# Where the batches of the second expert table, the norms and the routing pieces stand in a two-block transformer kernel on one core

## The reference, cut to what matters

```
qp = h @ w_pq;  sc = qp . sub_keys                 # 8 heads, 2 x 128 keys
s1, i1 = top_k(sc[0], 16);  s2, i2 = top_k(sc[1], 16)
top_s, top_c = top_k(s1[:, None] + s2[None, :], 16)
expert = e1 * 128 + e2                             # 8 x 16 rows of 16384, for each token
gate = softmax(top_s)
u = peer_u[expert];  w = gate * gelu(h . u)        # first table
y = sum(w * peer_v[expert])                        # second table
```

## Time and profile before

| | us |
|---|---|
| median of 3 runs | 2858.24 |
| lowest, highest | 2852.95, 2862.33 |
| the profiled execution | 2858.05 |
| its span, first to last instruction | 2856.2 |
| end of half 1's dense work on TensorE (last `key_scores`), in the trace | 2021.9 |
| windows of the last three rows of Rows 2 | `pq` of half 0, `pq` of half 1, `band` of half 0 |

### The profile page before, as it was taken

How to read it: one execution, slowest core, us unless ns; L and a number is a source line. 1 busy time by engine, 2 the same in 40 slices (tenths; PEclk the granted TensorE clock), 3 DMA queues, 4 the chain that set the end, 5 groups by cost and what they waited for, 6 DMA issues and landing times.

```text
span 2856.2 us, 26891 instructions
## 1 busy us (share of the span) xinstructions
PE 2056.2 (72%) x9570; PEld 1438.5 (50%) x9570; DVE 1378.4 (48%) x3142; ACT 417.0 (15%) x1058; POOL 1103.9 (39%) x1089
## 2 busy tenths in 40 slices
PE   8899899999889859786989999888520013323555
PEld 6788688876558648664767754446300000000111
DVE  3210256013327998966664345114479977564100
ACT  2311221012422122112000113311100000000000
POOL 1000011000003445545554543432565557777665
PEclk9899989989779969988999989989755556555677
DMA  6254359434227969988999987876787789999998
GB/s 232 74 155 141 103 208 347 152 96 133 71 89 290 348 229 342 348 318 323 362 406 349 384 310 288 292 279 225 285 327 281 289 303 363 363 364 370 384 361 329
DMA packets 214727, 779.13 MB, mean 273 GB/s; under 512 B 23892, under 2 KB 26516, under 8 KB 213572
## 3 DMA queue, kind: packets, MB, share of 16 engines
q0 software_dynamic: 155136, 564.97, 52.6%
q1 hardware_dynamic: 57272, 207.44, 20.6%
q10 hardware_dynamic: 2187, 5.01, 0.5%
HBM read 770.75 MB, written 6.58 MB: 272 GB/s over the span
## 4 chain that ended last, share of the span: by engine, by line
PE 52%; issue 15%; POOL 15%; DVE 11%; DMA 4%; ACT 2%; another core or an unknown queue 1%; ACTq 0%; DVEq 0%; POOLq 0%; SPq 0%
PE bank L546 39%; POOL main L489 15%; PE bank L710 4%; PE bank L649 2%; PE bank L665 2%; DMA main<-in_peer_v,idxT 2%; PE bank L614 2%; DMA main<-in_peer_u,idx 1%; DVE main L1405 1%; PE bank L656 1%; DVE small L1362 1%; PE bank L622 1%; DVE dots L1405 1%; DVE small L1359 1%
## 5 line engine op out<-in xcount | busy, mean ns | idle before, releaser
L546 PE MATMUL bank<-main,ring 128*128 128x256 f32 x4864 | 1085.3, 385 | 40.3 <-DVE main L1558 16.4
L546 PEld LDWEIGHTS bank<-main,ring 128*128 128x128 f32 x4864 | 932.6, 193 | 199.8 <-issue 45.1
L489 POOL DMA_INDIRECT main<-in_peer_v,idxT x512 | 527.6, 1031 | 499.0 <-PE bank L710 312.2
L489 POOL DMA_INDIRECT main<-in_peer_u,idx x512 | 539.8, 1054 | 465.3 <-DVE dots L1405 192.7
L710 PE MATMUL bank<-main,score_a 128*32 128x512 f32 x2048 | 358.8, 816 | 407.6 <-DMA main<-in_peer_v,idxT 377.0
L710 PEld LDWEIGHTS bank<-main,score_a 128*32 128x32 f32 x2048 | 73.7, 133 | 655.5 <-issue 654.3
L1405 DVE CUSTOM_DVE_ANT_0 main<-main 128x1024 f32<-128x1024 f32 x256 | 313.7, 1225 | 186.1 <-DMA main<-in_peer_u,idx 171.7
L1405 DVE CUSTOM_DVE_ANT_0 main<-main,h_a 128x1024 f32<-128x1024 f32 x256 | 313.6, 1225 | 97.2 <-DMA main<-in_peer_u,idx 69.3
L969 ACT ACTIVATE main<-bank 128x256 f32<-128x256 f32 (+4 forms) x346 | 146.6, 439 | 870.6 <-PE bank L546 708.1
L546 PE MATMUL bank<-ring,main 128*128 128x512 f32 (+3 forms) x624 | 239.4, 543 | 1.8 <-DMA ring<-in_w_stream 1.1
L482 POOL DMA_DIRECT2D main<-in_w_ada x48 | 25.5, 536 | 447.2 <-DVE main L1578 447.2
(11 more groups left out here) (221 smaller groups left out, 1363.5 us busy)
## 6 DMA issues: line engine op xcount, KB each, us to landing
ring<-in_w_stream SPq DMA_DIRECT2D x370, 512.0 KB
main<-in_w_ada POOLq DMA_DIRECT2D x48, 512.0 KB, 7.4
main<-in_peer_u,idx POOLq DMA_INDIRECT x512
main<-in_peer_v,idxT POOLq DMA_INDIRECT x512
main<-in_sub_keys SPq DMA_DIRECT2D x2, 1024.0 KB, 9.3
main<-rows_d SPq DMA_DIRECT2D x1, 1536.0 KB
main<-in_xT ACTq DMA_DIRECT2D x1, 1024.0 KB, 5.0
main<-in_memT POOLq DMA_DIRECT2D x1, 1024.0 KB, 8.8
```

Of the source, the lines that this page charges most:

```text
L489: gp.indirect_dma_start(rows_buf[:, slot, :], None, table, bass.IndirectOffsetOnAxis(ap=where, axis=0)).then_inc(landed[slot], 16)
L546: ins = pe.matmul(o, lhsT, rhs, **kw)
```

## The change

- `HEAD, PAIR, TAIL` go from 2.3, 3.4, 1.9 to 2.6, 3.8, 2.2: dots and batches are planned farther apart.
- On TensorE a tick now looks `LATE` = 8 us behind the clock, and a new `fill()` looks `EARLY` = 14 us ahead of it. `fill()` stands in `spread` before the wait for `diag_ready`, in each attention behind the second score product, and in front of the wait for `h2_ready`. The first batch of each tile comes `FIRST` = 24 us later.
- On VectorE and ScalarE no expert work is put in inside a norm (`spread`, `norm_std`).
- `route(n)` becomes a generator of six pieces. A routing that stood whole behind dot 8 of sixteen now has a piece behind each of dots 6 to 11, each due 1.3 us after its dot.

```diff
-    HEAD, PAIR, TAIL = 2.3, 3.4, 1.9
+    HEAD, PAIR, TAIL = 2.6, 3.8, 2.2
...
+            LATE, EARLY = 8.0, 14.0
+
             def tick(us):
                 clock[0] += us
                 if experts_now[0] is not None:
-                    experts_now[0].until(clock[0])
+                    experts_now[0].until(clock[0] - LATE)
+
+            def fill():
+
+                if experts_now[0] is not None:
+                    experts_now[0].until(clock[0] + EARLY)
...
                 norms[0] += 1
+                fill()
                 pe.wait_ge(S["diag_ready"], norms[0])
...
                 sums(KB)
                 spread()
-                tick(8.0)
+                fill()
+                clock[0] += 8.0
...
+                        if i == 1:
+                            fill()
...
-                        yield pace.batch(CG * t + q)
+                        yield pace.batch(CG * t + q) + (0.0 if q else FIRST)
...
                 mark("h2")
-                tick(6.0)
+                clock[0] += 6.0
+                fill()
...
                 norms[0] += 1
-                evacuated(sums_out + 1)
+                ve.wait_ge(S["lin_evacuated"], sums_out + 1)
...
-                    route(r0)
-                    yield pace.dot(n0)
-                    route(r0 + 1)
+                    for r in (r0, r0 + 1):
+                        for _ in route(r):
+                            yield pace.dot(n0)
+                    routing = None
...
-                        if j % TOPK == 8 and n // TOPK + 2 < r0 + TH * HEADS:
-                            route(n // TOPK + 2)
+                        if j % TOPK == 6 and n // TOPK + 2 < r0 + TH * HEADS:
+                            routing = route(n // TOPK + 2)
+                        if j % TOPK >= 6 and routing is not None:
+                            yield pace.dot(n) + 1.3
+                            next(routing, None)
```

More of the change, by code:

```diff
@@ L713, in combine @@
                 last.then_inc(S["v_used"], 1)
+            FIRST = 24.0
             def experts():
@@ L958, in _, with ready @@
             lin = [0]
-            def ready(n=1):
+            def ready(n=1, between=True):
                 lin[0] += n
-                experts_now.until(pace.lin[lin[0] - 1])
+                if between:
+                    experts_now.until(pace.lin[lin[0] - 1])
                 ac.wait_ge(S["lin_ready"], lin[0])
@@ L980, in norm_std @@
                 norms[0] += 1
-                b = ready()
+                b = ready(between=False)
                 if norms[0] > 1:
```

12 lines of the change are left out of this document (11 added, 1 removed).

## The result

| | before | changed |
|---|---|---|
| median, us | 2860.28 (4 runs) | 2916.22 (4 runs) |
| lowest, highest | 2852.95, 2865.84 | 2905.73, 2922.46 |
| ratio | | 1.0192, 95% interval 1.0169 to 1.0214 |
| the profiled execution, its span | 2858.05, 2856.2 | 2922.46, 2920.4 |
| end of half 1's last key scores | 2022.0 | 2033.2 |

The change costs 1.9%. Forecast were 2876 us: slower, as it came out, but the time lies 40 us above it and 14 above the range. In the profiled executions dense work ends 11.2 us later and the part behind it is 52.9 us longer.

A forecast was written before the change was run, and what follows sets the result against it. VectorE was taken to set the pace up to `out`, gathers and routings the end. Dense work ending 35 us earlier and 53 us more gathering gave 2858.05 - 35 + 53 = 2876 us, range 2843 to 2902.

The forecast's parts named there:

- Term 1: Half 1 up to `out`: fewer dots and one routing fewer due on VectorE shorten TensorE's waits, -30 us.
- the 92%: VectorE's busy share up to `out`, taken as too saturated for splitting the routing to gain anything there.
- Term 2: Later routings and bursts: shorter wait at `down` (-6), `mem` net -1; -7 us in all.
- Term 3: Batches' own TensorE time: six batches leave dense work (-11.5), one is covered in a norm (-2); -13 us.
- Term 4: TensorE waits for second-table rows in `norm2`, `cq`, `h2` and `o2`; +20 us, bounds +8 to +30.
- Term 5: `pq`: 18 half 1 gathers no longer run beside its weight stream; -5 us.
- Term 6: Behind dense work: 37 more gathers are left to do; +53 us, bounds 46 to 60.
- Sum 15 + 4 + 6 + 12 - 16.6: New row waits in `norm2`, `cq`, `h2`, `o2`, less the old row waits that go: +20 us.
- the term's own rule: New waits come wherever three or four batches stand in a row, since only two batches' rows are held.
- A: Rival, faster: VectorE stops being late up to `out`, waits in `mem`, `cq` and `o2` go; 2845 us, chance 0.20.
- B: Rival, no change: half the 37 gathers is hidden or dense work ends 50 us earlier; about 2858, chance 0.20.
- C: Rival, clearly slower: gathers take longer where weights stream; 2898 us, chance 0.12.

The follow-up runs named there:

- e3: Kernel before with only the routing split into six pieces; 2833.21 us, ratio 0.9912.
- e1: Kernel before with only the slower pace (HEAD, PAIR, TAIL 2.6, 3.8, 2.2); 2860.45 us, ratio 1.0005.
- e14: Changed kernel without its TensorE placement (LATE and FIRST 0, fills empty); pace, norms and pieces kept; 2866.08 us, ratio 0.9979 to the kernel before.
- e4: Kernel before with only expert work kept out of norms on VectorE and ScalarE; 2859.86 us, ratio 0.9991.
- e15: Changed kernel with old PAIR and TAIL, LATE and FIRST 0, fills kept; 2837.69 us, ratio 0.9882 to the kernel before.
- e13: The changed kernel itself, measured again in a later sitting; 2916.99 us, ratio 1.0168 to the kernel before.
- e12: Changed kernel with FIRST = 0 alone, LATE and fills kept; ratio 1.0053 to the kernel before.
- e10: Changed kernel with LATE and FIRST 0, fills kept; ratio 1.0006 to the kernel before.
- e17: Changed kernel without the fill behind the attentions' second score product, other fills kept; 2898.41 us, ratio 1.0115 to the kernel before.
- e18: Changed kernel with fills only in the attentions, none in norms or at h2; 2911.97 us, ratio 1.0177 to the kernel before.
- e2: Changed kernel with the old pace (HEAD, PAIR, TAIL 2.3, 3.4, 1.9); 2909.93 us, ratio 1.0185 to the kernel before.
- e11: The same kernel as e14, run in a sitting with faster gathers; 2809.06 us, ratio 1.0042 to the kernel before.

## Why the prediction was right or wrong

**Term 1, up to `out`: right in size, in part by luck.** `out` ends 33.3 us earlier (1247.8 to 1214.5), a batch (1.9) of it moved on: 31.4 for 30.4. The wait in `norm0`, which I said would nearly stay, went from 10.9 to 6.9. VectorE does 103 dots up to there for the 119 of the earlier trace rows. But the sentence "The six pieces alone bring nothing here" was wrong. The stretch takes 327.3 us before, 321.3 with the pieces alone (e3), 299.5 with the pace alone (e1) and 293.3 with both and the norms (e14), and the norms alone change nothing (e4, 327.4). So the pace is worth 27.8 us, 25.9 without the batch, and the pieces the other 6, against the 92%. Here the sentence of the Trainium skill that I set aside (Perfetto Trace Analysis, Optimizing Scalar/DVE Operations) was nearer to the trace than my reading of it.

**Term 2: right in kind in `down`,** which became shorter by more than its wait of 8.2 us: 11.9 us, of which a batch 1.9, for 6 forecast; e3 has it at 10.6 alone. `mem` kept its waits (11.7 us idle for 13.2), as the sum said.

**Term 3, one batch short.** Dense work holds 47 batches, not 48, as one more comes due right behind the last key scores: seven have left it, 13.4 us for the 11.5 of the sum.

**Term 4, the waits for rows: right in `norm2`, `o2` and `h2`.** In `norm2` TensorE idles 16.2 us more (23.5 for 7.3) for 15 forecast, with a wait before batch 3 and VectorE standing at its dot for 24.65 us. `o2` has 10.9 of idle time for 12, `h2` 3.8 more for 6. In `cq` the wait of 4 didn't come (1.3 us idle); `norm3` idles 3.3 us more, of which 0.86 for rows.

Waits for rows grew by 31.1 us (47.7 for 16.6). By the Trainium skill (DMA: Bandwidth & Descriptors, Anatomy of one DMA) term 4 would have been +8, which is further from that than my +20.

**Term 5: right.** `pq` holds five batches (9.6 us) and takes 75.3, which leaves 65.7 for its own work, that is 6.2 less than before for 5 forecast.

**Term 6, +53: right.** Measured 52.9. Half 1's first u gather is issued 34.1 us after the last key scores (2067.33) and v 224 58.3 after them (2091.54), for 33 and 55 in the forecast, and both are seen in the timeline of GpSimd:

```profile
2066.09 0.93 POOL L489 DMA_INDIRECT main<-in_peer_v,idxT  x1 [0.30 <-issue]
2067.33 0.94 POOL L489 DMA_INDIRECT main<-in_peer_u,idx  x1 [0.30 <-issue]
...
2091.54 1.56 POOL L489 DMA_INDIRECT main<-in_peer_v,idxT  x1 [0.30 <-issue]
```

e1 and e15 show that it belongs to `PAIR` and `TAIL`: 56 us with them, 55 less without.

**What failed: the end of dense work, 1987, by 46 us, and in it the step "Sum 15 + 4 + 6 + 12 - 16.6", a list of places in which `mla` and `fox` were missing.** I had seen that a fill stands behind the second score product, but priced four batches in `mla` and two in `fox` only as batches that are no longer there. By the sum these two and `fturn` should have become some 17 us shorter (nine batches fewer at 1.92); they became 26.6 longer. That is 44 of the 46 us: 11.0 of added waits, and some 33 by which TensorE took longer over the same work, at a lower granted clock. The repetition of the changed kernel (e13) has the same 152.6 us over these stages; without the placement (e14) they take 119.2 at the same pace, with three batches more in them. The runs show two things in place of the missing term:

- The batch drawn into the start waits for its rows (5.78 us in `mla`), as the term's own rule would have said had I asked it there. It is `LATE` that makes it wait: e12, with `LATE` = 8, has a wait of 5.66 us in front of that batch, and e10, which differs in `LATE` alone and ran beside it, has none. Without it (e17) there are 6.3 and 4.5 us less of waits in the two stages. How much of the rest comes through dots that are late on VectorE was not taken apart.
- TensorE then runs at the lower level though it is busy. e14 and the changed kernel do the same `mla` (275 and 274 instructions): 46.61 us busy at 0.90 against 59.53 at 0.69, so 12.9 of the 24.6 us between them are clock and 11.7 waits. What brings the clock down is open; by e18, e12, e2 and e10 it is not the waits alone. The forecast took every duration at the clock that its row had, and in the earlier trace rows stood a stage at 0.77 beside others at 0.95.

The Trainium skill has this as a rule (TensorE: Matmul & The Clock Gate, HAM oscillation — how this bites in real kernels): a wait for data drops the clock and what follows starts at half speed. The trace of the changed kernel agrees as to the fall: 1.00 from 1715 to 1725 us, 0.67 from 1735 to 1745 and 0.50 behind that. That it stays at 0.50 for 40 us (1745 to 1785) with TensorE busy for 10.00 of 10 us in two of the rows is more than the rule says.

The rivals: A and B died with the wait in `norm2` and in the attentions. C named the right side and 2898, but by longer gathers; its +5 on `o2` and +7 on term 6 did not come. What stays open: why the same code is granted different clocks. `fox` of one kernel took 70.7 us at 0.66 (e11) and 61.2 at 0.83 (e14), so a single trace gives that stage to some 10 us only. What rests on medians of one sitting is firmer: the placement costs 51 us.

## What to carry to other kernels

Before work is drawn ahead into a wait, ask whether its operands can be there at that moment: what is drawn ahead of a queue that has itself been made late becomes the wait. A pace that takes work off a busy stretch must say where that work goes; here `HEAD` with the pieces kept the gain (0.9802), and `PAIR` and `TAIL` paid it back behind the dense work. A stage whose filler work changes has to be priced at the lower clock too: `mla` and `fox` were granted anything from 0.62 to 1.00 in these runs, and a duration read from one trace holds for the clock of that trace only.
